# Twelve projection units of a hybrid decoder layer moved from direct products beside two recurrences into block-product pairs, and reloaded from DRAM

## The reference, cut to what matters

```python
proj = h @ w_in
(qa, fa, ia, ga, qb, kb, vb, ob, igb, fgb, bc, cc, xc, ad, gd, gates) = jnp.split(proj, ...)
forget = lb + (1.0 - lb) * sigmoid(fa)
log_fa, k_a, q_a, v_a = log(forget), 1.0 - forget, silu(qa), ia          # 4 heads of 128
o_a, s_hgrn_new = hgrn2_recurrence(q_a, k_a, v_a, log_fa, s_hgrn)        # branch A
o_a = head_rms_norm(o_a, norm_hgrn) * silu(ga)
q_b, k_b, v_b = qb * DK_B ** -0.5, kb, vb                                # 4 heads of 128
h_b, c_new, n_new, m_new = mlstm_recurrence(q_b, k_b, v_b, i_pre, log_fb, s_c, s_n, s_m)
o_b = sigmoid(ob) * head_rms_norm(h_b, norm_mlstm)                       # branch B
# two convolution branches from bc, cc, xc, ad, gd; then
gate = sigmoid(gates.reshape(bt, t, N_BRANCH, D_MODEL))
merged = jnp.sum(gate * jnp.einsum('btnc,ncd->btnd', branches, w_branch), axis=2)
```

## Time and profile before

| | us |
|---|---|
| median of three runs | 2180.22 (2179.70 to 2180.59) |
| the profiled execution: its time | 2176.39 |
| the profiled execution: its span, first to last instruction | 2174.6 |
| mean granted clock of PE | 0.998 of full |
| DMA traffic | 239.89 MB, mean 110 GB/s |

### The profile page before, as it was taken

How to read it: one execution, slowest core, us unless ns; L and a number is a source line. 1 busy time by engine, 2 the same in 40 slices (tenths; PEclk the granted TensorE clock), 3 DMA queues, 4 the chain that set the end, 5 groups by cost and what they waited for, 6 DMA issues and landing times. The chain is left out here.

```text
span 2174.6 us, 34482 instructions
## 1 busy us (share of the span) xinstructions
PE 2151.3 (99%) x13883; PEld 2035.9 (94%) x13883; DVE 1243.4 (57%) x1855; ACT 696.5 (32%) x1152; POOL 1103.8 (51%) x1329
## 2 busy tenths in 40 slices
PE   8999999999999999999999999999999999999998
PEld 7999999999999999999999999889999998888877
DVE  8522221799755435543453365658566667788775
ACT  5444442333231111242222121335333333333332
POOL 4444443778442333232234454710556658789880
PEclk9999999999999999999999999999999999999999
DMA  5233332121221121132242555323354446644432
GB/s 188 91 100 101 100 101 84 40 59 50 64 90 47 34 61 53 43 86 82 81 132 96 189 177 180 128 73 109 121 174 151 135 152 225 209 134 130 142 117 83
DMA packets 212787, 239.89 MB, mean 110 GB/s; under 512 B 14434, under 2 KB 156838, under 8 KB 212619
## 3 DMA queue, kind: packets, MB, share of 16 engines
q1 hardware_dynamic: 209745, 227.38, 33.0%
q0 software_dynamic: 2304, 8.91, 1.1%
q10 hardware_dynamic: 578, 1.38, 0.2%
HBM read 169.37 MB, written 68.64 MB: 109 GB/s over the span
## 5 line engine op out<-in xcount | busy, mean ns | idle before, releaser
L2202 POOL TENSOR_TENSOR w_lo<-w_raw,w_hi 128x256 fp32r<-128x256 f32 x490 | 380.6, 806 | 413.6 <-ACT w_hi L1719 413.0
L1166 PE MATMUL acc<-h_hi,w_hi 128*128 128x368 f32 (+2 forms) x1696 | 552.5, 326 | 0.5 <-issue 0.5
L1168 PE MATMUL acc<-h_hi,w_lo 128*128 128x368 f32 (+2 forms) x1696 | 546.5, 322 | 0.0
L1167 PE MATMUL acc<-h_lo,w_hi 128*128 128x368 f32 (+2 forms) x1696 | 546.0, 322 | 0.0
L1166 PEld LDWEIGHTS acc<-h_hi,w_hi 128*128 128x128 f32 x1696 | 318.5, 188 | 5.3 <-issue 4.0
L1167 PEld LDWEIGHTS acc<-h_lo,w_hi 128*128 128x128 f32 x1696 | 318.7, 188 | 0.0
L1168 PEld LDWEIGHTS acc<-h_hi,w_lo 128*128 128x128 f32 x1696 | 318.5, 188 | 0.0
L1719 ACT ACTIVATE w_hi<-w_raw 128x1024 fp32r<-128x1024 f32 (+2 forms) x162 | 141.5, 875 | 341.3 <-PE acc L1168 215.2
L2202 POOL TENSOR_TENSOR w_lo<-w_sum,w_hi 128x256 fp32r<-128x256 f32 x156 | 125.9, 832 | 134.0 <-ACT w_hi L1719 129.0
L1166 PE MATMUL pz<-t_op,w_hi 128*128 128x272 f32 x648 | 186.7, 288 | 0.3 <-POOL w_lo L2202 0.3
L1167 PE MATMUL pz<-t_op,w_hi 128*128 128x272 f32 x648 | 186.7, 288 | 0.0
(11 more groups left out here) (509 smaller groups left out, 4914.9 us busy)
## 6 DMA issues: line engine op xcount, KB each, us to landing
w_raw<-in_w_in SPq DMA_DIRECT2D x70, 512.0 KB, 4.1
a_raw<-down_operands SPq DMA_DIRECT2D x49, 512.0 KB, 3.8
gate_values<-staging SPq DMA_DIRECT2D x29, 544.0 KB, 3.7
gsig<-gate_values SPq DMA_DIRECT2D x29, 544.0 KB, 3.6
down_operands<-v_sums SPq DMA_DIRECT2D x14, 1024.0 KB, 4.4
w_raw<-in_w_up SPq DMA_DIRECT2D x18, 512.0 KB, 5.1
b_raw<-branch_outputs POOLq DMA_DIRECT2D x16, 544.0 KB, 5.5
w_raw<-in_w_branch SPq DMA_DIRECT2D x16, 512.0 KB, 4.7
```

The costliest lines, as they stand in the source:

```text
L1166: pe.matmul(out, lh, rh, start=first, stop=False, skip_group_check=more)
L1167: pe.matmul(out, lh, rl, start=False, stop=False, skip_group_check=more)
L1168: return pe.matmul(out, ll, rh, start=False, stop=last, skip_group_check=more)
L2202: return pool.tensor_tensor(out, x, y, op)
```

## The change

Twelve units, chosen over three heads of each recurrence (`KEPT`: fa of heads 1 and 2; qa, fa and ga of head 3; qb and kb of heads 1 to 3; ob of head 2), leave the stages 3 and 4. `pairs` grows from 13 to 19 pairs and computes them there, stores them behind the gates in `gate_values`, and SP loads each whole unit straight into the recurrence's own tile (`kept_load`) ahead of its head. In their place `ITEMS` has a "kept" item: for qa and ga a sigmoid on ACT and a multiplication on DVE over 1088 columns, for the others a mere signal. The recurrence stages are set anew around the units that stay: `a_two` between two feat units for A's heads 0 and 1, `a_value` beside the value units for A's head 2, `b_at` beside one feat unit for B's head 0, B's head 1 and 2 around `value("vb", 1)` and the unit ob 3. POOL's `spread_v` moves from `prep` to `turn`, and `state` on PE waits for the values. The first unit behind the pairs has weight tiles of its own (`w_first`).

```diff
-PAIRS = 13
+KEPT = (("fa", 1), ("fa", 2), ("qa", 3), ("fa", 3), ("ga", 3), ("qb", 1), ("kb", 1),
+        ("qb", 2), ("kb", 2), ("ob", 2), ("qb", 3), ("kb", 3))
+PAIR_UNITS = [("gt", (q // 8, q % 8)) for q in range(3, 29)] + list(KEPT)
+PAIRS = len(PAIR_UNITS) // 2
...
-    b_third = [0, 0.2, 0.38, 0.46, 0.6, 0.62, 0.75, 1]
+    a_two = [0.03 + i / 13 for i in range(8)] + [0.68, 0.76, 0.84, 0.86, 0.94, 1]
+    b_first = [0.03, 0.3, 0.5, 0.7, 1]
+    b_value = [0.05, 0.3, 0.5, 0.55, 0.85]
+    b_third = [0, 0.2, 0.5, 0.55, 0.85]
...
-            out += groups(unit("feat", nm, h))
+            out += [("kept", nm, h)] if (nm, h) in KEPT else groups(unit("feat", nm, h))
...
-    items += [("rec", "A", "prep", 0)] + merge(heads(a_names, 1), rec("A", 0, a_stages), a_at)
-    items += [("rec", "A", "prep", 1)] + merge(heads(a_names, 2), rec("A", 1, a_stages), a_at)
-    items += value("ia", 1)
-    items += [("rec", "A", "prep", 2)] + merge(heads(a_names, 3), rec("A", 2, a_stages), a_at)
+    items += [("rec", "A", "prep", 0)] + kept(a_names, 1) + merge(heads(a_names, 1), rec("A", 0, a_stages), a_two)
+    items += [("rec", "A", "prep", 1)] + kept(a_names, 2) + merge(heads(a_names, 2), rec("A", 1, a_stages), a_two)
+    a_value = [0.03 + 0.11 * i for i in range(8)] + 6 * [1]
+    items += [("rec", "A", "prep", 2)] + kept(a_names, 3) + \
+        merge(value("ia", 1) + heads(a_names, 3), rec("A", 2, a_stages), a_value)
...
-    items += [("rec", "B", "prep", 0)] + merge(heads(b_names, 1), rec("B", 0, b_stages), b_at)
-    items += [("rec", "B", "prep", 1)] + merge(heads(b_names, 2), rec("B", 1, b_stages), b_at)
-    items += value("vb", 1)
-    rec2 = rec("B", 2, b_stages)
-    items += [("rec", "B", "prep", 2)] + merge(heads(b_names[:2], 3), rec2[:7], b_third[:7])
+    items += [("rec", "B", "prep", 0)] + kept(b_names, 1) + merge(heads(b_names, 1), rec("B", 0, b_stages), b_at)
+    rec1, rec2 = rec("B", 1, b_stages), rec("B", 2, b_stages)
+    items += [("rec", "B", "prep", 1)] + kept(b_names, 2) + merge(heads(b_names, 2), rec1[:5], b_first)
+    items += [("rec", "B", "prep", 2)] + merge(value("vb", 1), rec1[5:] + rec2[:2], b_value)
+    items += kept(b_names, 3) + merge(heads(b_names, 3), rec2[2:7], b_third)
...
-    last = heads(b_names[2:], 3) + gates(0, 1, 2)
+    last = gates(0, 1, 2)
...
+            def kept_load(name, h):
+                if name[1] == "a" and h == 1:
+                    sp.wait_ge(sem("conv_done"), FT)
+                    sp.wait_ge(sem("ends_turned"), 1)
+                elif name[1] == "a":
+                    sp.wait_ge(sem("a_gated"), h - 1)
...
+                elif h == 1:
+                    sp.wait_ge(sem("b_rows"), 1)
+                else:
+                    sp.wait_ge(sem("b_gated"), h - 1)
...
+                sp.dma_start(kept_tile(name, h), parked[8 * M_IT + KEPT.index((name, h))]) \
+                    .then_inc(sem(f"buffer_in{KEPT_IN[name[0]]}"), 16)
...
+            def kept(name, h):
+                k, x = KEPT_IN[name[0]], name[1]
+                act.wait_ge(sem(f"buffer_in{k}"), 16 * (len(kept_before(name, h)) + 1))
...
+            def kept(name, h):
+                if name in ("qa", "ga"):
+                    dve.wait_ge(sem("a_proj"), 9 * h + (3 if name == "qa" else 9))
+                    tt(kept_tile(name, h), kept_tile(name, h), (ka if name == "qa" else sga)[:, h % 2, :], ALU.mult) \
+                        .then_inc(sem("a_silu"), 3)
```

More of the change, by code:

```diff
@@ L85, with kept_before @@
 M_IT, GS = 4, 3
-PAIRS = 13
+KEPT = (("fa", 1), ("fa", 2), ("qa", 3), ("fa", 3), ("ga", 3), ("qb", 1), ("kb", 1),
+        ("qb", 2), ("kb", 2), ("ob", 2), ("qb", 3), ("kb", 3))
+PAIR_UNITS = [("gt", (q // 8, q % 8)) for q in range(3, 29)] + list(KEPT)
+PAIRS = len(PAIR_UNITS) // 2
+PARKED = [8 * idx[0] + idx[1] if name == "gt" else 8 * M_IT + i - 26 for i, (name, idx) in enumerate(PAIR_UNITS)]
+KEPT_IN = {"q": 0, "f": 1, "k": 1, "g": 2, "o": 2}
+KEPT_N = [16 * sum(KEPT_IN[name[0]] == k for name, _ in KEPT) for k in range(3)]
+def kept_before(name, h):
+    return [u for u in KEPT[:KEPT.index((name, h))] if KEPT_IN[u[0][0]] == KEPT_IN[name[0]]]
 OPS_G, SUMS_G = 7 * PAIRS, 4 * PAIRS
@@ L182, in heads, with kept @@
                 out.append(("rec", "A", "prepq", h))
-            out += groups(unit("feat", nm, h))
+            out += [("kept", nm, h)] if (nm, h) in KEPT else groups(unit("feat", nm, h))
         return out
+    def kept(names, h):
+        return [("keptload", nm, h) for nm in names if (nm, h) in KEPT]
     def value(name, p):
@@ L295 @@
 F_IN = V_IN[0] + 16 * VP, V_IN[1] + 16 * VP
-BUFFERS_IN = [16 * len(range(GS + k, 8 * M_IT, GS)) for k in range(GS)] + [16 * H, 16 * H, 32 * H]
+BUFFERS_IN = [KEPT_N[k] + 16 * len(range(GS + k, 8 * M_IT, GS)) for k in range(GS)] + [16 * H, 16 * H, 32 * H]
 SUMS_D = SUMS_G + 4 * VP
@@ L410, in build @@
             v_sums = sb(st, "v_sums", [P, 4, 512])
+        with ExitStack() as st:
+            sb(st, "pad_w", [P, 95232 // 4])
+            w_first = sb(st, "w_first", [P, 2, UNIT], F32R)
         with ExitStack() as st:
@@ L765, in made, with slot @@
             return EARLY[u, g][2] if (u, g) in EARLY else GROUPS[u] + g + 1
+        def slot(u):
+            return (w_first[:, 0, :], w_first[:, 1, :]) if u == LEAD else (w_hi[:, u % SLOTS, :], w_lo[:, u % SLOTS, :])
         def slot_free(u):
-            if LEAD <= u < LEAD + 2:
-                return sem("g_done"), 14 * PAIRS - 4 + 4 * (u - LEAD)
+            if u == LEAD + 1:
+                return sem("g_done"), 2 * max(n + 1 for n in range(OPS_G) if (n + 3) // 2 % 2 == u % SLOTS)
             return group_ready, max(made(u - 2, 2), GROUPS[u - 1]) if u == 2 else GROUPS[u - 1]
@@ L1880, in g_sigmoid @@
                 act.wait_ge(sem("g_dve"), 6 * j + done)
-                v = g_value(j, corner)
-                act.activation(v, v, ACT.Sigmoid).then_inc(sem("g_sig"), 1)
+                v, name = g_value(j, corner), PAIR_UNITS[2 * j + (corner == "21" or corner == "22")][0]
+                if name in ("gt", "fa", "ob"):
+                    act.activation(v, v, ACT.Sigmoid).then_inc(sem("g_sig"), 1)
+                elif name == "qb":
+                    copy(v, v, scale=QSCALE).then_inc(sem("g_sig"), 1)
+                else:
+                    act.nop().then_inc(sem("g_sig"), 1)
             def pairs():
@@ L2407, in _ @@
                                 pool.wait_ge(sem("a_tree"), 7 * h + i + 1)
+                    elif x == "A" and s == "turn":
                         pool.wait_ge(sem("va_ready"), 9 * (h // 2) + 9)
@@ L2421, in _ @@
                             pool.wait_ge(sem("b_rows"), 1)
+                    elif x == "B" and s == "turn":
                         if h:
@@ L3458 @@
     decays = nc.dram_tensor("decay_rows", (2, H, T), F32, kind="Internal").ap()
-    parked = nc.dram_tensor("gate_values", (8 * M_IT, P, T), F32, kind="Internal").ap()
+    parked = nc.dram_tensor("gate_values", (8 * M_IT + len(KEPT), P, T), F32, kind="Internal").ap()
     x1_kept = nc.dram_tensor("residual", (NT + 1, P, D), F32, kind="Internal").ap()
```

64 lines of the change are left out of this document (48 added, 16 removed).

## The result

The changed kernel takes **2266.8 us** (median of 4 runs, 2262.0 to 2272.3) against 2180.2 for the kernel before (4 runs, 2179.7 to 2180.6): ratio 1.0403, 95% interval 1.0388 to 1.0418. It is slower, as forecast, but by 86.6 us and not by 63, and it lies 6.8 us above the range. The profiled execution took 2263.7 us with a span of 2262.1, 87.5 more than the span before.

The account below looks back on a forecast made before the run. PE, busy for 2151.3 us, was taken to bound the kernel. Matmuls -15.7, waits +64.5 and clock +14 gave about +63 us: 2180.2 + 63 = 2243 us, forecast 2235 to 2252, range 2222 to 2260.

Parts of the forecast that it names:

- Part 1: PE's matmuls: twelve direct units leave (-142.2 us), six more pairs come (+126.5 us), -15.7 us in all.
- Part 2: Reloads and kept items: each 544 KB reload lands in 3.6 us, issued a head ahead, so cost 0.
- forecast 4.5: B's head 0: PE waits 4.5 us for the weights, which hang on the decay rows' DMA.
- the forecast's 4.4: B's head 1, stages back to back: PE waits 4.4 us for the weights after gating, decay, exp and product.
- rival 4: Late reloads: in B's head 1 exp starts about 3 us later, 2246 us; counted inside the forecast's 0.62.
- The waits, 64.5 us: Part 3: sum of PE's new waits in both recurrences, where halves no longer lie between the stages.
- the 7.6 us for `out` to `gate`: Branch A: the chain from `out` through ACT and DVE's scaling until `gate` can start takes 7.6 us.
- Rival 2: Stretched chains: DVE steps slowed beside POOL (+8) and a low clock (+23), 2260 us; chance 0.14.
- Head 2's 12.2: A's head 2: the last six stages stand behind the last value half with nothing between, 12.2 us of waits.
- head 3's 4.0: A's head 3: `lv0` waits for DVE's gating and silu, then POOL's two passes, less a short half: 4.0 us.
- the end's 5.9: After the recurrences: PE waits 5.9 us for POOL's split of branch A's output.
- Part 4: Clock drops behind idle times above 3.24 us, 2.85 us lost each: +14 us, bounds 0 and 23.

Follow-up runs that it names:

- edit on ScalarE: The changed kernel, but ScalarE no longer waits for the reloads of B's kept units; TensorE and VectorE wait where they read: 2257.8 us, ratio 1.0363.
- run with the long waits filled: The changed kernel with 12 to 28 dummy products, results not read, on TensorE ahead of its eight long waits: 2257.2 us, ratio 1.0376.
- run with dummies everywhere: The changed kernel with dummy products ahead of its long waits and 4 to 13 more ahead of shorter ones: 2250.0 us, ratio 1.0324.
- respaced kernel: The kernel before with only four units (q, f of A's head 3; q, k of B's) moved into pairs, stages set anew: 2176.2 us, ratio 0.9985.

## Why the prediction was right and wrong

**The bound and the products: right.** The pair costs 21.05 us, a unit 11.85; with four units moved the sum came out within 1 us. Part 1 of the prediction stands.

**The reloads, "cost 0": wrong for B.** Part 2 let a reload take a head's length, but ACT passes its wait for it in the order of its list, ahead of the exp of the same head. It also lands later than the 3.6 us of the earlier trace rows:

```profile
kqr<-gate_values SPq DMA_DIRECT2D x6, 544.0 KB, 6.5
```

In head 0, ACT gets past it at 1085.59, 8.9 us after the issue; the wait for the weights was 6.9 us, forecast 4.5. The edit on ScalarE took 2.3 of that. The decay rows landed 7.4 us after their issue in place of 5.4, but that isn't what set the wait: in the run with the long waits filled they landed in 5.8, with the same reloads beside them, and dummies and waiting were 6.8 us all the same. In head 1 the forecast's 4.4 met the measured 5.0 by luck: without ACT's hold that wait is 0.2 us. DVE's `decay` took 3.65 us, not 4.5, and PE's scores ahead of that wait took 3.5 us at a slow clock, which uses up waiting; how the rest of the 4.2 us divides is open. So errors cancelled in that line, and rival 4, taken as worth 3 us, was worth 4.8 us of waiting.

**The waits, 64.5 us: right in place, too small in size.** Measured in the changed kernel, idle time is 73.9 us with 2.0 of old idle in it, so the waits are 71.9. The gates of A's heads 0 and 1 are 7.8 and 7.7 against 5.7. The first step that failed is the 7.6 us for `out` to `gate`: it was read from the earlier trace rows, where nothing runs beside DVE's scaling, and it was 9.8 in these two heads, 821.16 to 830.95 in the first. With two units in a head in place of three, the next head's `ga` is complete earlier, and GpSimd's product meets the scaling. Rival 2 had DVE slowed by GpSimd, at 8 us in all, but in the level steps of the earlier trace rows. The Trainium skill, in "SBUF — State Buffer", section "Who interferes with whom", states that a VectorE instruction with both inputs in SBUF and a GpSimd instruction that reads SBUF exclude each other for the whole instruction, whichever came first. The trace agrees: GpSimd's product ends at 829.74, 2.41 us after DVE's scaling was issued, and 2.41 and 1.36 make 3.77 where 3.62 was measured. Head 2's 12.2 was 12.1, head 3's 4.0 was 3.7, the end's 5.9 was 5.8. A second wait of 0.8 to 0.9 us in the levels of A's heads 0 and 1 and 1.2 for `vb` were not in the sum.

**The clock, +14: the price of one wait right, the count wrong.** Each long wait alone costs 2.8 us more than its length, in the kernel before, three times over. The Trainium skill ("TensorE: Matmul & The Clock Gate", section "HAM oscillation — how this bites in real kernels") has the price paid at every pause; these runs agree. The second step that failed is which waits pay it. Part 4 counted idle times above 3.24 us only, eight of them, and charged five in full. The products came out 24.7 us longer, above even its upper bound of 23. With just these eight filled they were still 15.1 us longer than at full clock (411.3 against 396.2): more than half of the 24.7 stands behind waits of at most 3.2 us, to which Part 4 gave no price. Not all of it is time, 12.9 to some 17 us in the recurrences: where DVE or ACT ends last, a slow product only uses up waiting.

Of the 5.0 us behind them, 2.3 belong to the slow stretch that follows the end's wait: 28 products start in 6.8 us where the kernel before has 42.

```profile
1263.71:1270.51 6.80, 6.80 (x28) 6.80 (x29) 0.94 (x2) 0.00 (x0) 4.80 (x8) 0.66 0.39 137
```

```profile
1181.18:1187.98 6.80, 6.80 (x42) 6.80 (x42) 1.61 (x3) 1.41 (x2) 4.95 (x8) 1.00 0.13 35
```

The first of these is the changed kernel, the second the kernel before. Another 1.6 is a wait of 2.01 us ahead of the output projection (0.44 before); what makes it longer was not looked into.

**What this makes of the sum.** Added up as they stand in the changed kernel, the waits are 7.4 us above the forecast (71.9 against 64.5) and the lengthened products 10.7 (24.7 against 14): together the 18 us. Of the 7.4, A's gates are 4.1 and B's first weights 2.4. The run with dummies everywhere divides them otherwise, as slow products hide waiting. It takes 481.8 us where the forecast has 462.7 at full clock (540.4 - 142.2 + 64.5), 19.1 more. 7.4 of these are the waits as they stand. Some 2.6 are products still slowed: dummies take 62.6 us, counted from start to next start, which leaves 398.8 for PE's own. The other 9.1 are idle time and dummies, 83.0 us against 73.9: 4.3 of dummies that cost time themselves, 2.3 more for B's weights of head 1, 1.4 more for POOL ahead of A's head 3, and smaller ones both ways. So at full clock the waits are some 12 us longer than forecast (19.1 - 4.3 - 2.6), and the clock costs some 20 us, the 17 and the 2.6, where 14 were forecast; both are estimates. By either division both terms were too small.

The other 6.7 us lie outside: 1.7 in front of A and 5.0 behind B. The starts of the profiled executions scatter by more than the 1.7 (the first scores at 767.2 to 770.6).

**The range.** Rival 2 (2260) came nearest, with the clock at its upper price and slowed DVE steps together. Its steps beside POOL were the wrong ones, and its 0.14 was too little: nothing in the rows bounded what meets whom in a new order, or behind which waits the clock falls, and the range should have reached to 2275.

## What to carry to other kernels

An operation that looks like a bound engine's work can be the cover of a chain. Before moving it, measure the chain of each stage and move only what stands there beyond it. Here three units, 35.5 us of other products, hid the chain of a head of A, and two, 23.7 us, did not; four of twelve units could go.

A wait's price is its length plus the time that TensorE then runs slowly, and that second part counts only where TensorE ends last. Price it from a run, not from the lengthened products alone, which here were 24.7 us for 12.9 to 17 us lost. And count the short waits too.

A duration read from the trace holds for its neighbours of that moment. When an order changes, ask for each step of a chain what will now run on the engine that shares its memory access, and which queue (here ScalarE's) is passed by a wait for a transfer.

## What the runs showed of the hardware

- VectorE's scaling of 128x1152 took 1.36 us alone and 3.62 beside GpSimd's product of 128x1088, which took 2.48 us in both cases and had started 0.07 us earlier: the later one paid.
- The granted clock can fall behind a wait much shorter than the 3.24 us of the earlier trace rows, and need not. In the run with ScalarE free, dense products and 16 level products stand ahead of a wait of 1.39 us, and the next 16 take 3.18 us in place of 1.89:

```profile
785.03 1.89 PE L1416 MATMUL pz<-proj_a 128*128 128x64 f32 x16
788.31 3.18 PE L1416 MATMUL pz<-proj_a 128*128 128x64 f32 x16 [1.39 <-DVE proj_a L2639]
```

Behind the same 1.39 us the changed kernel's head 1 took 2.00 us for its 16. The respaced kernel with its waits of at most 0.9 us kept 1.00 in the recurrences.

- A reload of 544 KB landed 6.5 us after its issue in branch B (median of six), where the gates' reloads of the same size took 3.7.

- Executions of one kernel differ in the clock and, with it, in time: five of the run with the long waits filled have mean clocks of 0.992 to 0.986 and take 2250.9 to 2265.0 us. The kernel before, at 0.996 to 1.000, scatters by 5 to 6 us only. A kernel with many waits is also harder to measure.
